# Moving small tiles and the rotary tables of a hybrid encoder layer so that the large on-chip tiles begin at multiples of 512 bytes

## The reference

```python
x = x + 0.5 * swiglu_ffn(x, ffn1_norm, ffn1_w_in, ffn1_w_out)        # 2048 -> 2 x 5632 -> 2048
h = rms_norm(x, mix_norm); proj = h @ w_in                           # 2048 -> 6144
a_q, a_k = partial_rope(rms_norm(a_q, ...)), partial_rope(rms_norm(a_k, ...))   # 8 heads, dilated windows
b_q, b_k = partial_rope(rms_norm(b_q, ...)), partial_rope(rms_norm(b_k, ...))   # 8 heads, differential
x = x + concat(rms_norm(a_o), rms_norm(b_o)) @ w_out                 # 2048 -> 2048
x = x + 0.5 * swiglu_ffn(x, ffn2_norm, ffn2_w_in, ffn2_w_out)
```

## Time and profile before

| | |
|---|---|
| median of 3 runs | 1810.41 us (1810.40 to 1810.42) |
| profiled execution | 1810.82 us, its span 1809.1 us |
| busy in the span | PE 1796.2, PEld 1480.3, DVE 1519.6, ACT 1119.2, POOL 79.0 us |
| granted PE clock | 0.999 |
| DMA | 378.62 MB, mean 209 GB/s |

### The profile page before, as it was taken

One profiled execution on the slowest core, in us unless ns is written; L12 is line 12 of the kernel. 1 busy time (PEld: TensorE's weight loads), 2 busy tenths in 40 slices (PEclk: granted clock), 3 DMA queues, 4 the chain that ended last, 5 costly groups with the idle time before them and its releaser, 6 DMA issues.

```text
span 1809.1 us, 21560 instructions
## 1 busy us (share of the span) xinstructions
PE 1796.2 (99%) x8167; PEld 1480.3 (82%) x8167; DVE 1519.6 (84%) x1676; ACT 1119.2 (62%) x1437; POOL 79.0 (4%) x113
## 2 busy tenths in 40 slices
PE   9999999999999999999999999999999999999999
PEld 7788888888888888888888888788888888888887
DVE  7999999899799887667766666899999999889986
ACT  7676666676665554556656654666667666656453
POOL 0000000000000000111010000000000000000000
PEclk9999999999999999999999999999999999999999
DMA  9777777776547566655455446577777766554653
GB/s 361 222 243 246 224 225 232 232 225 186 186 171 248 187 216 209 200 171 164 163 163 187 150 165 246 170 246 242 249 229 241 249 217 203 175 186 164 242 198 140
DMA packets 184199, 378.62 MB, mean 209 GB/s; under 512 B 7824, under 2 KB 8864, under 8 KB 183840
## 3 DMA queue, kind: packets, MB, share of 16 engines
q1 hardware_dynamic: 178304, 351.02, 56.0%
q0 software_dynamic: 5760, 26.22, 7.5%
q10 hardware_dynamic: 32, 0.01, 0.0%
HBM read 348.91 MB, written 2.10 MB: 194 GB/s over the span
## 4 chain that ended last, share of the span: by engine, by line
PE 98%; DVE 1%; DMA 0%; issue 0%; DVEq 0%; ACT 0%; SPq 0%
PE acc L590 27%; PE acc L595 13%; PE acc L654 12%; PE turn L673 10%; PE acc L673 7%; PE acc L659 6%; PE turn L677 5%; PE acc L677 4%; PE turn L796 3%; PE acc L796 2%; PE turn L624 1%; PE turn L799 1%; PE acc L799 1%; PE turn L915 1%; PE turn L590 1%; PE turn L936 1%
## 5 line engine op out<-in xcount | busy, mean ns | idle before, releaser
L1052 ACT ACTIVATE w_hi<-b 128x1024 fp32r<-128x1024 f32 (+1 forms) x300 | 267.1, 915 | 156.3 <-PE acc L659 122.2
L1447 DVE TENSOR_TENSOR w_lo<-b,w_hi 128x1024 fp32r<-128x1024 f32 (+1 forms) x300 | 300.0, 1042 | 57.7 <-ACT w_hi L1052 55.0
L1437 DVE TENSOR_TENSOR w_lo<-w_raw,w_hi 128x1024 fp32r<-128x1024 f32 x159 | 195.2, 1238 | 120.0 <-ACT w_hi L1028 119.5
L1028 ACT ACTIVATE w_hi<-w_raw 128x1024 fp32r<-128x1024 f32 x158 | 166.9, 1060 | 184.5 <-PE acc L595 169.2
L1066 ACT ACTIVATE w_hi<-w_raw 128x1024 fp32r<-128x1024 f32 x184 | 194.2, 1060 | 140.1 <-PE acc L595 97.1
L1457 DVE TENSOR_TENSOR w_lo<-w_raw,w_hi 128x1024 fp32r<-128x1024 f32 x184 | 223.2, 1222 | 42.1 <-ACT w_hi L1066 38.6
L590 PE MATMUL acc<-w_hi,h_hi 128*128 128x512 f32 x496 | 196.4, 396 | 0.0
L590 PE MATMUL acc<-w_hi,h_lo 128*128 128x512 f32 x496 | 193.2, 390 | 0.0
L590 PE MATMUL acc<-w_hi,act_hi 128*128 128x512 f32 x480 | 188.2, 392 | 0.0
L590 PE MATMUL acc<-w_hi,act_lo 128*128 128x512 f32 x480 | 188.1, 392 | 0.0
L654 PE MATMUL acc<-w_hi,h_hi 128*128 128x512 f32 x480 | 187.2, 390 | 0.0
(11 more groups left out here) (235 smaller groups left out, 3433.9 us busy)
## 6 DMA issues: line engine op xcount, KB each, us to landing
b<-in_ffn_w_in SPq DMA_DIRECT2D x80, 1280.0 KB, 5.8
w_raw<-in_ffn_w_out SPq DMA_DIRECT2D x88, 1024.0 KB, 5.2
w_raw<-in_ffn_w_in SPq DMA_DIRECT2D x54, 1024.0 KB, 6.4
w_raw<-in_w_in SPq DMA_DIRECT2D x48, 1024.0 KB, 5.1
w_raw<-in_ffn_w_in SPq DMA_DIRECT2D x44, 512.0 KB, 6.4
w_raw<-in_w_out SPq DMA_DIRECT2D x16, 1024.0 KB, 5.0
b<-t POOLq DMA_DIRECT2D x20, 768.0 KB, 7.8
b<-t POOLq DMA_DIRECT2D x20, 512.0 KB, 4.6
```

The lines of the kernel that those rows point to most:

```text
L1028: nc.scalar.activation(w_hi[:, u % RING, 0:count, :], w_raw[:, slot, k0:k0 + count, :], ACT.Copy).then_inc(hi_ready, 1)
L1052: nc.scalar.activation(w_hi[:, u % RING, 0:count, :], in_raw(piece)[:, k0:k0 + count, :], ACT.Copy).then_inc(hi_ready, 1)
L1437: nc.vector.tensor_tensor(w_lo[:, slot, 0:count, :], w_raw[:, v // 2 % RAW, k0:k0 + count, :], w_hi[:, slot, 0:count, :].bitcast(F32), ALU ...
L1447: nc.vector.tensor_tensor(w_lo[:, u % RING, 0:count, :], in_raw(piece)[:, k0:k0 + count, :], w_hi[:, u % RING, 0:count, :].bitcast(F32), A ...
```

## The change

The six small tiles are allocated right behind the identity, which becomes a tile of its own (`ident_sb`); `root` shrinks from 72 to 56 columns. The rotary tables move to a tile of their own, `rope_sb`, among the tiles of the attention, whose space is used by other tiles in the feed-forward layers. Their load therefore moves: it is issued just ahead of the mask's, after the first group's weight loads, with a semaphore of its own, on which POOL waits before it makes `turns_a` and `turns_b`. The waits on `const_landed` count 16 loads in place of 17.

By the same placing rule `ident_sb` begins at 1152, `root` at 1664, the other small tiles at 1888 to 2024, and `x_sb` at 2048. So `x_sb` to `dump` and the identity stay where they were. `w_raw` and all that follows it begin 448 bytes earlier: `w_raw` at 103936, `t_1` at 128512, `act_hi` at 136704, all multiples of 512.

```diff
-        cst = sb("cst", [P, P + N_ROPE])
+        ident_sb = sb("ident_sb", [P, P])
+        root = sb("root", [P, 56])
+        sumsq = sb("sumsq", [P, TT, 4])
+        rstd = sb("rstd", [P, TT])
+        lam = sb("lam", [P, 4])
+        gain_col = sb("gain_col", [P, 4])
+        half_rstd = sb("half_rstd", [P, TT])
         x_sb = sb("x_sb", [P, TT, D])
...
         dump = sb("dump", [P, NC], mybir.dt.bfloat16)
-        sumsq = sb("sumsq", [P, TT, 4])
-        rstd = sb("rstd", [P, TT])
-        lam = sb("lam", [P, 4])
-        root = sb("root", [P, 72])
-        gain_col = sb("gain_col", [P, 4])
-        half_rstd = sb("half_rstd", [P, TT])
...
             norm_in = sb("norm_in", [KD, P], F32, attention)
+            rope_sb = sb("rope_sb", [P, N_ROPE], F32, attention)
...
-            sp.dma_start(cst[:, P:P + N_ROPE], consts[:, P + TT * SEQ:N_CONST]).then_inc(const_landed, 16)
...
                 if g == 0:
                     sp.wait_ge(units_used, UNIT[QKV])
+                    sp.dma_start(rope_sb[:, :], consts[:, P + TT * SEQ:N_CONST]).then_inc(rope_landed, 16)
                     sp.dma_start(mask[:, :, :], consts[:, P:P + TT * SEQ]
...
-                dve.wait_ge(const_landed, 16 * 17)
+                dve.wait_ge(const_landed, 16 * 16)
...
-            pool.wait_ge(const_landed, 16 * 17)
+            pool.wait_ge(const_landed, 16 * 16)
...
             pool.wait_ge(units_used, UNIT[QKV])
+            pool.wait_ge(rope_landed, 16)
```

More of the change, by code:

```diff
@@ L290, in hybrid_layer_kernel @@
         banks = acc + [turn[1][:, :].rearrange("p (t n) -> p t n", n=NC)]
-        ident = cst[:, 0:P]
-        at = P
+        ident = ident_sb[:, :]
+        at = 0
         rope = []
         for half in (16, 8):
-            table = cst[:, at:at + 2 * TT * half].rearrange("p (f t r) -> p f t r", f=2, t=TT)
+            table = rope_sb[:, at:at + 2 * TT * half].rearrange("p (f t r) -> p f t r", f=2, t=TT)
             rope.append((table[:, 0], table[:, 1]))
@@ L320, in hybrid_layer_kernel @@
         mask_landed = sem("mask_landed")
+        rope_landed = sem("rope_landed")
         gain_landed = sem("gain_landed")
```

## The result

| | before | after |
|---|---|---|
| median | 1810.41 us (1810.40 to 1810.68, 4 runs) | 1799.29 us (1799.22 to 1799.49, 4 runs) |
| span of the profiled execution | 1809.1 us | 1797.6 us |

The ratio is 0.9938, with a 95% interval of 0.9921 to 0.9956. The change made the kernel 11.1 us faster. The prediction had said 1810.4 us, with a range of 1809.0 to 1811.6 and a chance of 0.05 for faster.

The account below looks back on a forecast made before the run. PE, busy for 1796.2 of 1809.1 us, was taken as the bound. From 1810.82, -0.1 (first transfer), +0.1 (DVE in stalls), 0 and 0 gave 1810.8; the median stands 0.4 lower, so 1810.4 us, range 1809.0 to 1811.6.

Parts of the forecast that it names:

- the first point of Part 1: PE's matmuls with weights from tiles moved by 448 bytes: equal weight loads, 390 against 392 ns, so a gain of 0.
- Rival 2: Some engine is faster on aligned tiles: DVE 10% faster in stalls, 1807.2 us, or PE 2 ns per matmul, 1794; chance 0.07.
- DVE and ACT: Making `w_lo` and rounding from aligned or misplaced tiles: DVE 1225 against 1222 ns, ACT 1060 for both, so no gain.
- The +0.1 us of 3 ns in the stalls: Stalls at the start of both feed-forward layers: 14 DVE instructions, each perhaps 3 ns slower on aligned tiles, +0.1 us for both.
- Transfers: DMA into aligned tiles may become up to 5% faster; the whole gain, at the start-up, between 0 and 0.4 us.
- The 0.1 us that the sum gave to the first transfer: Start-up, first half block of weights: faster loading lets PE's first product begin earlier, taken as -0.1 us.
- Parts 2 and 3: One small load fewer at the start, others up to 2.56 us earlier; rotary tables landing at 749.2 to 754.3 us; both worth 0.
- What would show it: Signs in the profile after: PE busy 1796 us again; wrong if matmuls start under 229 ns apart, PE waits near 779, or stalls shrink.

Follow-up runs that it names:

- the kernel at 256: Changed kernel with 256 bytes of padding before `w_raw`, moving it and every tile behind it: 1799.34 us.
- the equal costs at 448, 192 and -64: 448: kernel before, 1810.41 us. 192: changed kernel, 192 bytes of padding before `w_raw`, 1810.46 us. -64: changed kernel, only `w_hi`/`w_lo` 64 bytes later, 1814.98 us.

## Why the prediction was wrong

**The step that failed** is the first point of Part 1: PE's price was set at 0, "the matmul 390 and 392 ns. Even if those 2 ns were real, they are the length of overlapping records". They were real. The rows held the effect with its right size, 2 ns, and I argued it away by the reading of a record's length. Overlap makes a record's length a poor measure of the rate; it does not make a steady difference between two groups of 496 and 480 mean nothing. The chain of before shows x8 in 1.83 us in the output stage (above) and in 1.81 in the first projection group, whose weights are `h`:

```profile
722.12 1.81 PE acc L590 x8
723.93 0.91 PE acc L595 x4
```

One such pair proves little, but here nearly all agree: in the output stage of before 52 of 55 such runs of eight take 1.83 us and none less, in the first projection group 19 of 21 take 1.81. That comparison needed no experiment. At PE's 99% share the measured 1.89 and 1.90 us on the 1692 matmuls on `act` of both layers are 3.8 us of the 11.1. The rest is 6.9 us in the rows of matmuls that hold `s_hi`, whose two groups of 240 had 398 and 401 ns beside 389 for `h_hi` in the same lines L673 and L677, and which I didn't look at, and 0.6 on `mix`.

**The question was wrong too.** I compared tiles "at a multiple of 512" with tiles 448 past one, as an absolute property of a tile, and noted that PE streams `w_hi` and `w_lo`, "which do not move", as if that made PE's moving side drop out. What counts is the distance between the two tiles that PE reads at a time. By luck the two came to the same here, since the moving tile stood at a multiple; with both off by 128 an absolute rule would have said slow and the chip was fast (72.54 us).

**Rival 2** came nearest to what happened ("If each of PE's 8167 matmuls gained 2 ns, 16 us: 1794") at 0.07 and for all matmuls; only those on `act`, `mix` and `s_hi` could gain. The groups of before would have given 2 to 3 ns on the 1692 matmuls on `act` (3.4 to 5.1 us) and, against 389 ns, 240 x 12 + 240 x 9 + 80 x 2 + 80 x 9 ns = 5.9 us on the four groups on `s_hi`: 1801.1 to 1799.4 us. That estimate is close to the 1799.3 measured, in part by luck: 397 and 391 ns remain in the two groups of 240 after the change, so part of the 12 and 9 ns was never the placing, and what makes up for it lies in groups that the estimate leaves out (`s_lo`, and `s_hi_more` with 394 before and 389 after). It still deserved more than 0.07.

**DVE and ACT** right: no gain from aligned reads. The rows after, against 1222 and 1225 in the earlier trace rows:

```profile
L1459 DVE TENSOR_TENSOR w_lo<-w_raw,w_hi 128x1024 fp32r<-128x1024 f32 x184 | 222.7, 1221 | 38.7 <-ACT w_hi L1068 35.7
L1459 DVE TENSOR_TENSOR w_lo<-rows,w_hi 128x1024 fp32r<-128x1024 f32 x34 | 41.6, 1224 | 8.5 <-ACT w_hi L1068 8.1
```

The +0.1 us of 3 ns in the stalls did not show: the difference of 3 ns between the two groups is still there with both tiles aligned, so it never was the placing.

**Transfers** right in direction and worth: 387 to 409 GB/s is 5.7%, and the kernel with only the weight buffers off has 387 again and the same time. Where all large tiles were moved by 32 or 128 bytes the rows show 387 and 388; where those from `w_raw` on were moved by 256 they show 408. The 0.1 us that the sum gave to the first transfer is not to be seen: the start took 53.61 us with only the weight buffers off, at 387 GB/s, and 53.93 with only `s_hi` off, at 409, against 53.97 before and 53.60 after.

**Parts 2 and 3** right: the kernel with the tables loaded early has the same time. The landing took 4.8 us (5.2 to 10.3 said), the turns 3.35 (3.22 said), and they ended at 746.6, before the 752.4 said, since the load was issued at 738.33 and not at 744.0; PE's transposes waited for nothing new.

**What would show it** worked as written: "The prediction is wrong if the 512-column matmuls start closer together than 229 ns". They do, at 227. But 229 was the pace of the output stages, on `act`, and on `h` the kernel before ran at 227 already. So the sign should have been asked of before's own stages. "PE busy for 1796 us again" failed as well, with 1785.5.

**Left open.** Which part of the on-chip memory or of PE makes two streams at a distance slower, and why 192 is cheap, no run here shows; the numbers give a pattern by distance, not a mechanism. Nor do they show why rows that mix distances cost what they do, nor where the 0.8 us come from that the kernel with all tiles moved by 128 has above the changed one. Whether the load of the next weights has to coincide with the stream, or something else joins the two tiles, was not tried. That the period is 256 rests on the kernel at 256 and on the equal costs at 448, 192 and -64.

## What to carry to other kernels

When PE is busy for 99% of a kernel, take the addresses of the tile it loads as weights and of the tile it streams, and make their difference a multiple of 256 bytes. In these runs a small tile in front of a large one cost up to 1.3% when it moved stationary tiles (0.6% in the kernel before) and 2.3% when it moved the tile that PE streams. A difference of 2 ns between two steady groups of the same shape is worth its count: multiply before dismissing it, and check it with the start-to-start rate of unbroken runs, not with a record's length. And when a trace seems to hold both placings already, ask which pair of operands each row stands for, since a property of a pair can't be read from one of them.

## What the runs showed of the hardware

- A 128x512 matmul in float32 parts started 226.7 ns after the one before it at a distance of 0 between its two tiles' beginnings (by 256 bytes), and later at others: by 2.2 ns at 192 and by 6.3 to 7.0 at 32, 64 and 128 in the output stage on `act`, by 2.2 and 5.5 at 192 and 128 in the first projection group on `h`. The weight loads stayed at 188 ns, PE was not idle in the stages compared, and the clock was 1.00.
- The slower pace is not confined to the misplaced tile: with `s_hi` alone at 192, matmuls on `s_hi_more`, at distance 0, right behind it were recorded with 394 to 395 ns in place of 389.
- The place of both tiles together is nearly free: 128 bytes off for all cost 0.8 us of 1799.3.
- With the DMA engines full, transfers into on-chip memory ran at 387 or 388 GB/s where destinations begin off a multiple of 256 bytes (32, 64, 128 or 192 past one) and at 408 to 409 where on one.
- Reads by DVE and ACT from tiles 192 bytes past a multiple of 256 cost nothing: the whole kernel took 1799.40 us with all weight buffers there, against 1799.29.
